# Retention's two units of a tile put in one slot, rotations placed behind the softmax norms, and one expert matrix loaded ahead of a wait

## The reference, cut to what matters

```
intra = einsum('bihd,bjhd->bhij', q, k) * decay
o     = einsum('bhij,bjhe->bihe', intra, v)
cross = einsum('bihd,bhde->bihe', q, S) * cross_scale
out   = o + cross
S_new = full * S + einsum('bjhd,bjhe->bhde', k * w, v)
```

## Time and profile before

| | |
|---|---|
| median of three runs | 565.93 us (565.28 to 566.42) |
| the profiled execution's own time | 561.45 us |
| its span, first to last instruction | 559.7 us |
| PE, DVE, ACT, POOL busy | 491.9, 265.0, 133.5, 155.6 us |
| bytes moved by transfers | 144.73 MB |

### The profile page before, as it was taken

How to read it: one execution, slowest core, us unless ns; L and a number is a source line. 1 busy time by engine, 2 the same in 40 slices (tenths; PEclk the granted TensorE clock), 3 DMA queues, 4 the chain that set the end, 5 groups by cost and what they waited for, 6 DMA issues and landing times.

```text
span 559.7 us, 7531 instructions
## 1 busy us (share of the span) xinstructions
PE 491.9 (88%) x2747; PEld 311.2 (56%) x2747; DVE 265.0 (47%) x595; ACT 133.5 (24%) x361; POOL 155.6 (28%) x279
## 2 busy tenths in 40 slices
PE   4976988998999999999994799969999869788974
PEld 4955766766776677778783654323343323233333
DVE  2869679885454555662225622322333221112535
ACT  4754354463547223232111100000000000000110
POOL 5446763041113654742104300211111210100003
PEclk9989998997999999999997799979999998889999
DMA  9440220220028902229939799999999999999997
GB/s 303 152 128 3 76 76 2 71 81 1 2 76 291 299 11 83 86 95 401 417 138 381 291 391 406 409 423 411 421 420 420 420 419 417 423 419 422 411 413 234
DMA packets 35030, 144.73 MB, mean 259 GB/s; under 512 B 5842, under 2 KB 8994, under 8 KB 23216
## 3 DMA queue, kind: packets, MB, share of 16 engines
q1 hardware_dynamic: 26320, 129.94, 59.2%
q0 software_dynamic: 4528, 9.01, 4.4%
q10 hardware_dynamic: 4144, 5.28, 2.8%
HBM read 138.16 MB, written 17.30 MB: 278 GB/s over the span
## 4 chain that ended last, share of the span: by engine, by line
PE 49%; DVE 14%; DMA 12%; SPq 11%; ACT 4%; issue 4%; ACTq 1%; DVEq 0%; POOLq 0%
PE banks L1059 17%; PE banks L1291 10%; SPq L723 7%; DMA w_moe_b<-in_w_up_dram 5%; PE banks L1306 4%; SPq L731 3%; DMA w_moe_b<-y_d 3%; DMA y_d<-rows,idx 2%; PE banks L1285 2%; DMA rows<-hn_d,idx 2%; PE banks L1207 1%; PE banks L1202 1%; DMA y_d<-y_sb,idx 1%; PE banks L1053 1%; PE banks L1241 1%
## 5 line engine op out<-in xcount | busy, mean ns | idle before, releaser
L880 POOL TENSOR_TENSOR w_lo<-w_raw,w_hi 128x512 fp32r<-128x512 f32 x52 | 69.9, 1358 | 115.8 <-ACT w_hi L1569 114.0
L1291 PE MATMUL banks<-w_moe_b,xgT 128*64 128x512 f32 x224 | 67.1, 619 | 10.7 <-DMA w_moe_b<-in_w_up_dram 7.1
L1291 PE MATMUL banks<-w_moe_a,xgT 128*64 128x512 f32 x224 | 67.9, 627 | 4.3 <-DMA w_moe_a<-in_w_up_dram 4.3
L1701 ACT ACTIVATE glu_a<-banks,wr 128x256 f32<-128x256 f32 x15 | 7.1, 474 | 196.2 <-PE banks L1291 183.4
L2235 DVE SCALAR_TENSOR_TENSOR glu_b<-banks,wr,glu_a 128x256 f32<-128x256 f32 x15 | 7.2, 483 | 96.9 <-ACT glu_a L1701 96.9
L1059 PE MATMUL banks<-w_hi,xT_hi_a 128*128 128x512 f32 (+3 forms) x124 | 50.9, 410 | 1.6 <-DVE xT_lo_a L1763 1.6
L1291 PEld LDWEIGHTS banks<-w_moe_b,xgT 128*64 128x64 f32 x224 | 21.1, 142 | 49.5 <-issue 46.5
L1059 PE MATMUL banks<-w_lo,xT_hi_a 128*128 128x512 f32 (+3 forms) x124 | 48.3, 390 | 0.0
L1059 PE MATMUL banks<-w_hi,xT_lo_a 128*128 128x512 f32 (+3 forms) x124 | 48.1, 388 | 0.0
L1059 PE MATMUL banks<-w_hi,xT_hi_b 128*128 128x512 f32 (+3 forms) x92 | 35.6, 387 | 0.8 <-issue 0.8
L1291 PEld LDWEIGHTS banks<-w_moe_a,xgT 128*64 128x64 f32 x224 | 21.4, 144 | 26.2 <-issue 24.2
(11 more groups left out here) (336 smaller groups left out, 924.7 us busy)
## 6 DMA issues: line engine op xcount, KB each, us to landing
w_moe_a<-in_w_down_dram SPq DMA_DIRECT2D x20, 1024.0 KB, 20.5
w_moe_a<-in_w_gate_dram SPq DMA_DIRECT2D x16, 1024.0 KB, 12.1
w_moe_a<-in_w_up_dram SPq DMA_DIRECT2D x16, 1024.0 KB, 14.6
w_moe_b<-in_w_gate_dram SPq DMA_DIRECT2D x14, 1024.0 KB, 17.0
w_moe_b<-in_w_up_dram SPq DMA_DIRECT2D x14, 1024.0 KB, 17.1
w_moe_b<-in_w_down_dram SPq DMA_DIRECT2D x10, 1024.0 KB, 26.0
w_raw<-in_w_in_dram SPq DMA_DIRECT2D x34, 256.0 KB, 4.2
y_d<-in_consts_dram SPq DMA_DIRECT2D x9, 512.0 KB, 9.7
```

What stands on the lines that cost most here:

```text
L880: nc.gpsimd.tensor_tensor(w_lo[:, s, :], w_raw[:, s, :], w_hi[:, s, :].bitcast(F32), ALU.subtract).then_inc(split, 1)
L1291: l = mm(acc[64 * e:64 * e + 64, u, :].rearrange("p (m f) -> p m f", m=2), xgT[:, xu, k, 64 * e:64 * e + 64], units(at_e[e], 2)[:, :, k * ...
```

## The change

- `plan()`: `("post", RQK, t)` moves from the end of the slot of its job to the head of the next slot's `before` list, and is put there after the `norm` steps; the norms of units 4, 7 and 10 now come ahead of the rotations of TAIL, tile 1 and tile 3 on DVE, and the rotation of SQ's tile 3 ahead of that of RQK's tile 0; tile 2's keeps its place. `counts` goes behind RQK's last rotation.
- `plan()`: the two `ra` of a tile stand at the end of the even slot r0 + 2i, the two `ro` at the end of the odd slot r0 + 2i + 1. `rm` of units 1, 3, 5, 6 and 7 goes from the head of its slot to its end.
- PE: the even unit's step only takes a bank; at the odd unit's step the products of both units are issued alternately: the two halves of the rows in `ra` and in the state's part, the two halves of the columns in the outer products. The products of scores and v use the whole array as before. TAIL's products keep their waits between one another.
- SP: the first of the two down matrices of pair 0 is issued before the wait for the gathered rows.

```diff
-    before[30] += [("counts",)]
...
-        behind[done(RQK, t)].append(("post", RQK, t))
...
+    for t in ORDER:
+        before[done(RQK, t) + 1].append(("post", RQK, t))
+    before[30] += [("counts",)]
...
-        after[r0 + m].insert(after[r0 + m].index(("ro", m - 1)) if m > 7 else len(after[r0 + m]), ("ra", m))
-        after[r0 + m + 1].append(("ro", m))
+        after[r0 + m // 2 * 2].append(("ra", m))
+        (after if m > 1 else behind)[r0 + m // 2 * 2 + 1].append(("ro", m))
...
-        after[r0 + late[m]].insert(0, ("rm", m))
+        after[r0 + late[m]].insert(len(after[r0 + late[m]]) if m in (1, 3, 5, 6, 7) else 0, ("rm", m))
...
+            sp.dma_start(dn_at(0, 0), down_v[0]).then_inc(dn_in[0], 16)
             sp.wait_ge(xg_in[0], 16)
-            load_dn(0)
+            sp.dma_start(dn_at(0, 1), down_v[1]).then_inc(dn_in[0], 16)
...
+                ra_bank[par] = b
+                if par == 0:
+                    return
                 pe.wait_ge(rT_ev, nth["rT", t])
                 for hp in range(2):
-                    l = mm(sideA[0:R, b, P * hp:P * hp + R], rT[hs, r, 2 + hp, 0:R], rT[hs, r, hp, 0:R],
-                           start=True, stop=True)
-                l.then_inc(ra_ps, 1)
+                    for half in range(2):
+                        hs = slice(64 * half, 64 * half + 64)
+                        l = mm(sideA[0:R, ra_bank[half], P * hp:P * hp + R], rT[hs, r, 2 + hp, 0:R], rT[hs, r, hp, 0:R],
+                               start=True, stop=True)
+                        if hp:
+                            l.then_inc(ra_ps, 1)
...
-                outer(0, R, t, par, b)
+                for hp in range(2):
+                    for half in range(2):
+                        l = outer(0, R, t, half, ro_bank[half], hp)
+                        if hp:
+                            l.then_inc(st_ps, 1)
...
+                if R == P:
+                    for hp in range(2):
+                        for half in range(2):
+                            of_scores(half, hp)
+                        for half in range(2):
+                            l = of_state(half, hp)
+                            if hp:
+                                l.then_inc(ro_ps, 1)
+                    return
```

More of the change, by code:

```diff
@@ L1159, in value, with outer @@
                 busy[b] = [(o_hi, i + 1), (o_lo, i + 1)]
[L1161 to L1168, removed]
+            def outer(lo, n, t, par, b, hp):
+                h = 2 * hp + par
+                return mm(sideA[64 * par:64 * par + 64, b, P * hp:P * hp + P],
+                          rqk[lo:lo + n, t, 256 + 64 * h:256 + 64 * h + 64],
+                          rv[lo:lo + n, t, P * h:P * h + P], start=True, stop=True)
             def meta_state(par, b):
@@ L1173, in meta_state @@
                 pe.wait_ge(posted, nth["post", RQK, TAIL])
-                outer(DEC, NMETA, TAIL, par, b)
+                for hp in range(2):
+                    l = outer(DEC, NMETA, TAIL, par, b, hp)
+                l.then_inc(st_ps, 1)
                 busy[b] = [(st_new, st_nth["meta_state", par])]
+            ra_bank, ro_bank = {}, {}
             def ret_scores(m, b):
@@ L1179, in ret_scores @@
                 R = out_rows(t)
-                hs, r = slice(64 * par, 64 * par + 64), ORDER.index(t) % 2
+                r = ORDER.index(t) % 2
                 take(b)
+                ra_bank[par] = b
+                if par == 0:
+                    return
                 pe.wait_ge(rT_ev, nth["rT", t])
                 for hp in range(2):
-                    l = mm(sideA[0:R, b, P * hp:P * hp + R], rT[hs, r, 2 + hp, 0:R], rT[hs, r, hp, 0:R],
-                           start=True, stop=True)
-                l.then_inc(ra_ps, 1)
+                    for half in range(2):
[4 more added lines that the diff above has]
+                            l.then_inc(ra_ps, 1)
             def ret_out(m, b):
@@ L1191, in ret_out @@
                 state = state_s if t == TAIL else state_p
-                hs, r = slice(64 * par, 64 * par + 64), ORDER.index(t) % 2
+                r = ORDER.index(t) % 2
+                ro_bank[par] = b
+                if par == 0:
+                    return
                 pe.wait_ge(ra_ev, m + 1)
                 pe.wait_ge(acc_free, job_of(RV, t) + 1)
-                outer(0, R, t, par, b)
-                if t != TAIL:
-                    pe.wait_ge(st_new, st_nth[("ro", m - 2) if t else ("meta_state", par)])
@@ L1199, in ret_out @@
[L1199 to L1210, removed]
@@ L1211, in ret_out, with of_scores @@
-                l.then_inc(ro_ps, 1)
+                for hp in range(2):
+                    for half in range(2):
+                        l = outer(0, R, t, half, ro_bank[half], hp)
+                        if hp:
+                            l.then_inc(st_ps, 1)
+                if t != TAIL:
+                    for half in range(2):
+                        pe.wait_ge(st_new, st_nth[("ro", m - 3 + half) if t else ("meta_state", half)])
+                def of_scores(half, hp):
+                    h = 2 * hp + half
+                    return mm(sideA[0:R, ro_bank[half], 2 * P + P * hp:2 * P + P * hp + P],
+                              ret_aT[0:R, (m - 1 + half) % DEEP, hp, 0:R], rv[0:R, t, P * h:P * h + P],
+                              start=True, stop=False)
@@ new lines, in of_state @@
+                def of_state(half, hp):
+                    hs = slice(64 * half, 64 * half + 64)
+                    return mm(sideA[0:R, ro_bank[half], 2 * P + P * hp:2 * P + P * hp + P], rT[hs, r, hp, 0:R],
+                              state[hs, hp, :], start=False, stop=True)
+                if R == P:
+                    for hp in range(2):
+                        for half in range(2):
+                            of_scores(half, hp)
+                        for half in range(2):
+                            l = of_state(half, hp)
+                            if hp:
+                                l.then_inc(ro_ps, 1)
+                    return
@@ L1213, in ret_T @@
+                for half in range(2):
+                    for hp in range(2):
+                        of_scores(half, hp).then_inc(ro_part, 1)
+                        pe.wait_ge(ro_part, 2 * (m - 1 + half) + hp + 1)
+                        l = of_state(half, hp)
+                        if hp == 0:
+                            l.then_inc(ro_cross, 1)
+                            pe.wait_ge(ro_cross, m + half)
+                    l.then_inc(ro_ps, 1)
             def ret_T(m, b):
```

## The result

The changed kernel takes 559.4 us (median of 20 runs), the kernel before 564.8 (20 runs); the ratio is 0.9922, 95% interval 0.9900 to 0.9944, that is 4.4 us faster. The time lies inside the forecast range, near its upper end, but only a third of the 13.4 us came. The profiled execution took 559.13 itself, its span is 557.3.

What follows compares the result with a forecast made beforehand. TensorE bounds retention and the output projection, transfers the end of the expert stage. 6.0 + 6.0 + 1.5 = 13.5 us off the profiled 561.45 gives 548.0; with 4.5 to the median, stated as 552.5, range 547.5 to 560.5.

Steps and rivals of the forecast that it cites:

- Part 1: Attention, rotations behind norms on VectorE: 6.0 us gained, bounds 3.0 and 9.0.
- the second place: Attention, unit 10's transposition at 127.81: TensorE's 3.07 us wait and the slow clock behind it go, 6.1 us gained.
- TensorE would ask for it at about 130: Attention, unit 11's norm: delayed until about 127.7 to 128.7 in the old clock, still ahead of TensorE's need.
- the first place: Attention, transposition at 89.03: its 1.85 us wait goes, but TensorE waits for unit 6's norm instead; 0.4 us gained.
- rival (c): Attention: stall returns at unit 11's transposition, or clock falls again at unit 6; attention gives 2 us, 556.5; chance 0.16.
- Part 2: Retention's units in pairs: products, waits and TAIL sum to 6.5 us gained, taken as 6.0; bounds 3.0 and 8.5.
- the sum of the products: Retention on TensorE: 3.46 us a tile, four tiles 13.8, which is 7.3 us less than today's 21.1.
- two state renewals and sums, then a norm: VectorE behind a pair in retention: norm ends 3.9 us after next job's start; TensorE waits some 0.4 us each time.
- TAIL's pair saves about 0.4: Retention, TAIL's two units issued as a pair: about 0.4 us gained, though their products still wait for one another.
- Part 3: Expert stage, first down matrix issued before the gathered rows: 1.5 us gained, bounds 0 and 2.4.
- TensorE has about 0.4 us to spare there: Expert stage, at the gather: it may come some tenths later, within TensorE's slack of about 0.4 us.
- as long as the queue doesn't run dry: Expert stage: condition for the early matrix to count at the end; at 336 the queue holds about 2 us of work.

Runs made afterwards that it cites:

- i1_no_down: The changed kernel with only the first down matrix put back behind the wait for the gathered rows; ratio to the kernel before 0.9900.
- f2_norms_sooner: f1_base with VectorE's norms of the odd units and unit 6 put ahead of the next state renewals; ratio to the kernel before 0.9772.
- e3_down: The kernel before with only the first down matrix issued ahead of the wait for the gathered rows; ratio 1.0035.
- f1_base: The changed kernel with only tile 3's rotation and counts behind the norms, and the down matrix back behind the gathered rows; ratio to the kernel before 0.9856.
- f4_tail_apart: f1_base with TAIL's two units in slots of their own again, the four tiles still in pairs; ratio to the kernel before 0.9867.
- h1_two_down: f1_base with both down matrices of pair 0 issued ahead of the wait for the gathered rows; ratio to the kernel before 0.9935.
- e2_pairs: The kernel before with retention's units in pairs alone, rotations and down matrix as before; ratio 0.9937.
- e4_last_rotation: The changed kernel with only tile 3's rotation and counts behind the norms, the other rotations back in their old places; ratio to the kernel before 0.9896.
- f3_rotations_late: f1_base with the rotations of TAIL and tiles 0 and 1 moved ten slots and more back; ratio to the kernel before 0.9829.
- g2_tail_paired: f1_base with the changes of f2_norms_sooner and f3_rotations_late, unit 0's transposition at its slot's end, TAIL's units still paired; ratio to the kernel before 0.9751.

## Why the prediction was wrong

By the stages 3.9 us came of the 13.5 of the sum: 4.35 are missing in retention, 2.9 in the expert stage and 2.4 in attention. Each part has a step that failed.

**Part 1: the second place was right.** From RV's second TAIL half to tile 0's second half it took 14.87 us before and 8.56 after (121.75 to 136.62, 124.93 to 133.49): 6.3 returned, 6.1 were forecast. Where "TensorE would ask for it at about 130" no wait came, but 0.94 at ScalarE's copy for the same unit 11 (137.46). That wait is most of the 1.0 that the rest of the stage lost (37.36 to 38.36).

**The step of part 1 that failed** is "at the first place I count almost nothing ... 0.4 us is left". The prediction saw that VectorE has no pause from 84 to 101 and that TensorE would wait for unit 6's norm, and took the new wait to cost no more than the old. The old place cost 1.85 and 1.3 in a slow job behind it (6.60 against 5.26 after). The new one cost 2.26, 1.05 in `score` and 1.8 in the job. From RQK's tile 0 to RV's second TAIL half the stretch became 1.7 us longer (40.98 to 42.66). This is rival (c) in kind, "a second fall of the clock at unit 6", given 0.16; it had 2 us for all of attention, and 3.6 came. The fall is not in every execution: in the profile of i1_no_down, with the same order of work and the same wait of 2.26, `score` took 1.20 and the job 3.0, and the granted clock from 105 to 110 was 1.00 instead of 0.50. So the wait that moved is certain, and the clock behind it makes it dearer in some runs.

**Part 2: the sum of the products was right, its terms were not.** A tile costs 2.72 + 0.64 = 3.36 where 3.46 was forecast. The eight outer records took 189.21 - 188.62 = 0.59, 74 ns each, where I had 60. The Trainium skill's page "TensorE: Matmul & The Clock Gate", Part 3, has weight loads overlap running products only where the row group differs. The prediction had drawn 145 ns for column halves on the same rows from that; 74 ns speak against it, as `value` did. The state's eight took 2 x 0.42, 105 ns each, where I had 75 from `score`. That is half of the 210 before. "TensorEngine Tiling (Array Packing)" of the Trainium skill, Overview, gives at most 2x for halves, and this row agrees. Scores took 2 x 0.64, 160 ns, where I had left them at 210.

**What failed there is the waits**, the largest single miss: 1.2 at units 1, 3 and 5 forecast and 2.5 found, and at OUT0's transposition nothing forecast and 1.8 found. The 0.3 for the splits came as forecast (0.30 at 227.70). The chain was right in kind: "two state renewals and sums, then a norm". It was 3.9 in the forecast and ended 195.79 - 191.34 = 4.45 after the job's start, because VectorE begins only 0.58 after it, once ScalarE's squares are there, and the eight steps then take 3.0. At OUT0 I had priced only the splits on POOL, not the transposition of unit 6, whose norm has the same place behind two renewals; the job behind that wait also took 1.3 us more. And "TAIL's pair saves about 0.4" cost 1.0: its products still wait for one another, all of them together took 4.19 us (175.09 to 179.28), the granted clock fell (0.68 from 178 to 180, 0.50 from 180 to 182), and the job behind them took 4.25 instead of 2.98. With these terms the sum of 6.5 becomes 6.5 + 0.4 - 1.3 - 1.8 - 1.3 - 1.4 = 1.1, against 1.65 found; a wait of 0.45 at L1230 that only before has (238.81) is most of the rest. f2_norms_sooner shows that the waits at the odd transpositions were a matter of order, not a price of pairing.

**Part 3: the wrong sign.** "TensorE has about 0.4 us to spare there" was the step: in e3_down the rows were transposed 4.89 us after the gather's issue instead of 4.41, TensorE stood idle for 0.32, and the two steps behind it ran at a granted clock of 0.50 and 0.84 (before, 1.00); the next load came 1.5 us later. The condition that the prediction set itself, "as long as the queue doesn't run dry", failed too: the loads that follow wait for buffers that TensorE frees, so the pause of the transfers at 314 was not removed but came back 10 us later, at 324 to 326. Both causes stood beside the bound of 0, but nothing excluded that they cost more than nothing.

Two readings of that part were off without deciding it. In e3_down SP issued the matrix at 306.30, not "at about 302", and before, the transfers moved 4.9 MB between 302 and 313.5 (422 GB/s), not 7. In the slices of the earlier trace rows the long run of nines begins with the nineteenth, not the eighteenth.

The range held the time because its upper end took in (c) and the low bounds of two parts: that is its width, not a sum that came true. Three signs named for being wrong did come: a new wait at L1131's step for another unit (2.26), one over 1 us at L1219's step (1.78), and a pause of transfers near 336 (share 0.53 from 334 to 336 after).

## What to carry to other kernels

Where an engine is full over a whole stretch, changing the order by one place moves the stall to the next asker; take the work to where the engine has room, and follow the first waiter behind the new place before counting a gain. When two results are made to arrive together, put what is already ready ahead of their consumers in each in-order queue: here that alone gave 4.7 us, more than the 3.6 that the pairing by itself had kept. A large transfer slipped in ahead of a small one that an engine waits for was paid twice here, by the wait and by the clock behind it, and it gained nothing, since later transfers waited for buffers.

## What the runs showed that I had not expected

VectorE operations with both inputs in SBUF were held up by POOL's splits of weights. The 1.62 us of the earlier trace rows, which the prediction used without a cause, is one: POOL's split ran from 126.04 to 127.31. Three more, from the timelines of POOL and of VectorE after, with the 1.76 us at 92.42 shown above for the first (the split of 5.19 us is four in a row):

```profile
92.01 1.63 POOL L882 TENSOR_TENSOR w_lo<-w_raw,w_hi 128x512 fp32r<-128x512 f32 x1 [0.34 <-ACT w_hi L1604]
...
200.30 1.27 POOL L882 TENSOR_TENSOR w_lo<-w_raw,w_hi 128x512 fp32r<-128x512 f32 x1 [0.18 <-POOL root_r L305]
...
222.46 5.19 POOL L882 TENSOR_TENSOR w_lo<-w_raw,w_hi 128x512 fp32r<-128x512 f32 x4 [0.18 <-POOL root_r L305]
```

```profile
200.32 1.53 DVE L2082 TENSOR_TENSOR xT_lo_a<-part_r,xT_hi_a 128x256 fp32r<-128x256 f32 x1 [0.47 <-ACT xT_hi_a L1693]
...
224.96 1.54 DVE L2030 TENSOR_TENSOR state_p<-h_b,cst 64x256 f32<-64x256 f32 x1
```

Operations of the last two forms take 0.42 to 0.45 elsewhere, of the first 0.69. An operation that reads a bank of PSUM was not held up: L2029 at 224.50, amid the four splits, took its usual 0.42. "SBUF — State Buffer" of the Trainium skill, section "Who interferes with whom", says that a VectorE instruction with two inputs in SBUF contends with a GpSimd instruction that reads SBUF, and that the port pair they share is an exclusive lock; these rows agree. The 1.1 us lost at 224.96 lie in the chain of the longest wait (1.78). Ahead of unit 6's norm three operations after lost 3.0 us in this way (at 87.64, 90.56 and 92.42; before, three lost 2.9), more than the wait of 2.26 there. That the splits made either wait is argued and not tried.

Whether the clock falls behind a wait differs from one execution to the next. Behind the 1.85 us at the first place the job and what follows up to the next took 6.6 us in the profiles of before, f1_base, f4_tail_apart and h1_two_down and 5.0 in those of e2_pairs, e3_down, e4_last_rotation and f2_norms_sooner, with the same steps in the same order. Behind TAIL's pair the job and the `ra` after it took 5.5 to 6.5 us in after, e2_pairs, f1_base, f3_rotations_late, g2_tail_paired, h1_two_down and i1_no_down, and 4.2 in e4_last_rotation and f2_norms_sooner. What decides between the two was not found; it makes single profiles differ by 1.3 to 2.3 us at each such place, so a part's price is read from the waits, which repeat within some hundredths, and from many runs.
